# Six groups in the first set of an opening input projection: two retention jobs split 4 and 12 k tiles, one value job split 8 and 8

## What is computed

```python
mod = c @ w_ada[layer] + b_ada[layer]
sh1, sc1, gt1, sh2, sc2, gt2 = jnp.split(mod, N_MOD, axis=-1)
h = modulate(rmsnorm(x, g_mix[layer]), sh1, sc1)
proj = h @ w_in[layer]
...
qa, ka, va, qr, kr, vr, gr = jnp.split(proj, cuts, axis=-1)
ya = sliding_window_attention(qa, ka, va, sinks[layer]) * beta_attn[layer]
yr = retention(qr, kr, vr)
yr = (jax.nn.silu(gr) * head_group_norm(yr, g_ret[layer]))
y = jnp.concatenate([ya, yr], axis=-1) @ w_out[layer]
x = x + gt1[:, None, :] * y
h2 = modulate(rmsnorm(x, g_ffn[layer]), sh2, sc2)
f = jnp.square(jax.nn.relu(h2 @ w1[layer])) @ w2[layer]
x = x + gt2[:, None, :] * f
return rmsnorm(x, g_final)
```

## Time and profile before

| what | value |
|---|---|
| median of three runs | 1176.98 us |
| lowest, highest | 1175.03, 1178.56 us |
| span of the profiled execution (its time from first to last instruction) | 1176.1 us |
| TensorE busy | 1132.5 us, 96% of the span |
| VectorE busy | 795.4 us, 68% |
| ScalarE busy | 492.5 us, 42% |
| loaded from memory | 300.36 MB |

### The profile page before, as it was taken

The page is one execution under the profiler, slowest core; times in us unless marked ns, Lnnn a source line. Parts: engine busy times, 40 slices in busy tenths (PEclk is TensorE's granted clock), DMA queues, the critical chain, the costliest instruction groups (busy, mean ns, idle before and its releaser), DMA issues.

```text
span 1176.1 us, 15924 instructions
## 1 busy us (share of the span) xinstructions
PE 1132.5 (96%) x6339; PEld 957.8 (81%) x6339; DVE 795.4 (68%) x690; ACT 492.5 (42%) x517; POOL 21.1 (2%) x27
## 2 busy tenths in 40 slices
PE   3879999999999999999999999999999999999996
PEld 1769989788778878888888888888888888888885
DVE  2577889987878898866565566565566565565675
ACT  2424454555534445443333444333444333444451
POOL 2000010000000001000000000000000000000000
PEclk9999999999999998999999999999999999999999
DMA  9999989999997956766666676666676666665551
GB/s 351 368 348 397 381 319 339 338 403 390 357 404 269 322 182 223 252 222 229 235 230 185 188 222 228 235 228 186 187 220 229 238 224 187 187 196 180 180 177 72
DMA packets 156749, 303.10 MB, mean 258 GB/s; under 512 B 5425, under 2 KB 73633, under 8 KB 148129
## 3 DMA queue, kind: packets, MB, share of 16 engines
q1 hardware_dynamic: 155248, 298.08, 72.4%
q10 hardware_dynamic: 832, 2.93, 0.6%
q0 software_dynamic: 624, 1.48, 0.4%
HBM read 300.36 MB, written 2.10 MB: 257 GB/s over the span
## 4 chain that ended last, share of the span: by engine, by line
PE 91%; DVE 4%; DMA 3%; issue 1%; ACT 1%; ACTq 0%; SPq 0%; DVEq 0%
PE ps_job L924 20%; PE ps_job L963 14%; PE ps_job L964 14%; PE ps_job L965 14%; PE ps_job L927 10%; PE ps_job L939 3%; PE ps_job L940 3%; PE ps_job L941 3%; DMA stage<-in_w_ada 2%; PE ps L1030 1%; DVE acc L1247 1%; DVE w_lo L1323 1%; DMA cst<-in_consts 1%; PE ps_job L1211 1%; PE ps_job L1209 1%
## 5 line engine op out<-in xcount | busy, mean ns | idle before, releaser
L1323 DVE TENSOR_TENSOR w_lo<-stage,w_hi 128x2048 fp32r<-128x2048 f32 x164 | 375.8, 2292 | 218.5 <-ACT w_hi L518 218.3
L518 ACT ACTIVATE w_hi<-stage 128x2048 fp32r<-128x2048 f32 (+1 forms) x167 | 318.0, 1904 | 424.0 <-PE ps_job L965 231.4
L924 PE MATMUL ps_job<-act_hl,w_hi 128*128 128x512 f32 x1024 | 322.4, 396 | 1.5 <-DVE w_lo L1323 1.1
L927 PEld LDWEIGHTS ps_job<-act_hl,w_lo 128*128 128x128 f32 x1024 | 192.7, 188 | 45.0
L927 PE MATMUL ps_job<-act_hl,w_lo 128*128 128x256 f32 x1024 | 201.2, 278 | 0.0
L963 PE MATMUL ps_job<-w_hi,hid_hl 128*128 128x512 f32 x480 | 188.1, 392 | 0.0
L964 PE MATMUL ps_job<-w_lo,hid_hl 128*128 128x512 f32 x480 | 187.0, 390 | 0.0
L965 PE MATMUL ps_job<-w_hi,hid_hl 128*128 128x512 f32 x480 | 186.9, 389 | 0.0
L924 PEld LDWEIGHTS ps_job<-act_hl,w_hi 128*128 128x128 f32 x1024 | 156.1, 189 | 2.5 <-DVE w_lo L1323 1.3
L1247 DVE SCALAR_TENSOR_TENSOR acc<-stage,small,acc 128x2048 f32<-128x2048 f32 (+1 forms) x56 | 122.9, 2195 | 7.2 <-DMA stage<-in_w_ada 3.5
L963 PEld LDWEIGHTS ps_job<-w_hi,hid_hl 128*128 128x128 f32 x480 | 90.1, 188 | 19.2 <-issue 0.7
(11 more groups left out here) (223 smaller groups left out, 1127.1 us busy)
## 6 DMA issues: line engine op xcount, KB each, us to landing
stage<-in_w SPq DMA_DIRECT2D x128, 1024.0 KB, 5.3
stage<-in_w_ada SPq DMA_DIRECT2D x64, 1024.0 KB, 7.8
stage<-in_w_in SPq DMA_DIRECT2D x41, 1024.0 KB, 8.5
stage<-in_w_ada SPq DMA_DIRECT2D x32, 512.0 KB, 6.9
stage<-in_w_out SPq DMA_DIRECT2D x16, 1024.0 KB, 7.7
gate_rows<-in_w_ada SPq DMA_DIRECT2D x16, 1024.0 KB, 7.0
x_sb<-in_x ACTq DMA_DIRECT2D x1, 2048.0 KB, 13.5
out_y<-f_acc SPq DMA_DIRECT2D x3, 512.0 KB, 2.7
```

The source lines that it names most:

```text
L518: nc.scalar.activation(w_hi[:, ring, 0:width], stage[:, slot, 0:width], ACT.Copy).then_inc(hi_ready, 1)
L924: nc.tensor.matmul(ps_job[:, 2 * pair + e, :], w_hi[:, ring, ws], act_hl[:, kt, :], start=(kt == 0), stop=False)
L927: last = nc.tensor.matmul(ps_job[:, 2 * pair + e, T:2 * T], w_lo[:, ring, ws], act_hl[:, kt, 0:T], start=False, stop=(kt == KT - 1))
L1323: nc.vector.tensor_tensor(w_lo[:, ring, 0:width], stage[:, slot, 0:width], w_hi[:, ring, 0:width].bitcast(F32), ALU.subtract).then_inc(lo_ ...
```

## The change

The two wide jobs on the columns `QR0 + 512` and `QR0 + 1024` are cut at k tile 4 instead of 8: their first part is one group on k tiles 0 to 3 and moves into the first set, their second part is three groups on k tiles 4 to 15 in the second pass. The first set becomes g0 to g5: key and value, the two moved ones, then the two query jobs and `QR0`. The value job of full depth becomes two jobs of 8 k tiles, g18 and g19 of the first pass and g25 and g26 of the second; its single ACT copy becomes an ACT copy and a DVE add. Both passes keep their number of groups (20 and 23), and the number of wide and tok groups over both is unchanged (24 and 16); the first pass has two wide groups less and two tok groups more, the second pass the reverse. All tiles of the second segment now stand ahead of g5; the third segment is spread over 13 groups (g7 to g19) instead of 15. `sum_second` is called with h = g + 1 instead of g + 2, and no longer once ahead of the loop.

```diff
+SET_K = 4
+EARLY = (1, 2)
+def w_in_jobs(second):
+    k0 = HALF if second else 0
+    early = [("wide", QR0 + TOK_COLS * n, 0, SET_K) for n in EARLY]
+    jobs = [] if second else early
+    jobs += [("feat", KV0, k0, HALF)] + [("wide", Q0 + TOK_COLS * n, k0, HALF) for n in range(2)]
+    if second:
+        jobs += [("tok", VR0 + TOK_COLS, k0, HALF)]
+        jobs += [("wide", QR0 + TOK_COLS * n, SET_K, KT - SET_K) if n in EARLY else ("wide", QR0 + TOK_COLS * n, k0, HALF) for n in range(4)]
+    else:
+        jobs += [("wide", QR0 + TOK_COLS * n, k0, HALF) for n in range(4) if n not in EARLY]
     jobs += [("tok", GR0 + TOK_COLS * n, k0, HALF) for n in range(2)]
+    jobs += [("tok", VR0, k0, HALF)]
+    return jobs if second else jobs + [("tok", VR0 + TOK_COLS, k0, HALF)]
...
+FIRST_SET = [(j, 0) for j in [J_KV, *range(J_KV), *range(J_KV + 1, J_CLOSED)]]
+GROUPS = FIRST_SET + [(j, 1) for j in range(J_KV, J_CLOSED)] + [(j, q) for j in range(J_CLOSED, len(JOBS)) for q in range(N_GROUPS[j])]
+G_SET = len(FIRST_SET)
...
 def tiles_before(g):
-    second = min(KT, (0, 2, 6, 9)[g] if g < OPEN else KT)
+    second = (0, 1, 4, 7, 11, KT)[g] if g < G_SET else KT
...
-    return KT + second + min(KT, max(0, 16 * (g - OPEN) // 15)) + later
+    return KT + second + min(KT, max(0, 16 * (g - G_SET) // (G_B - 1 - G_SET))) + later
...
-            if j in (1, 2):
-                return [0, 1] if j == 1 else [4, 5]
-            if j in (0, OPEN - 1):
-                return [2] if j == 0 else [6, 7]
+            if j < J_CLOSED:
+                return [[0, 1], [4, 5], [2], [0, 1], [4, 5], [6, 7]][j]
...
-                if g - 2 == LAST_GROUP[J_V]:
-                    act.wait_ge(evacuated, J_V)
-                    act.wait_ge(group_used, LAST_GROUP[J_V] + 1)
-                    nc.scalar.activation(result_of(J_V), psum_of(J_V), ACT.Copy).then_inc(evacuated, 1)
...
             pe.wait_ge(mod_ready, 1)
-            sum_second(1)
...
-                if g + 2 <= OPEN:
-                    sum_second(g + 2)
+                if g < G_SET - 1:
+                    sum_second(g + 1)
```

More of the change, by code:

```diff
@@ L46 @@
 HALF = KT // 2
[L49 to L53, removed]
+SET_K = 4
[10 more added lines that the diff above has]
+        jobs += [("wide", QR0 + TOK_COLS * n, k0, HALF) for n in range(4) if n not in EARLY]
     jobs += [("tok", GR0 + TOK_COLS * n, k0, HALF) for n in range(2)]
-    return jobs + [("tok", VR0, k0, HALF)]
-JOBS = w_in_jobs(0, []) + w_in_jobs(HALF, [("tok", VR0 + TOK_COLS, 0, KT)])
+    jobs += [("tok", VR0, k0, HALF)]
+    return jobs if second else jobs + [("tok", VR0 + TOK_COLS, k0, HALF)]
+JOBS = w_in_jobs(False) + w_in_jobs(True)
 JOBS += [("out_attn", TOK_COLS * n, 0, HALF) for n in range(STRIPS)]
 JOBS += [("out_ret", TOK_COLS * n, HALF, HALF) for n in range(STRIPS)]
-J_B = len(w_in_jobs(0, []))
+J_B = len(w_in_jobs(False))
 J_BQ, J_BGR = J_B + 1, J_B + 8
 J_OA = J_BGR + 3
-J_V = next(j for j, job in enumerate(JOBS) if job[1:] == (VR0 + TOK_COLS, 0, KT))
 J_OR = J_OA + STRIPS
 J_MLP = J_OR + STRIPS
-OPEN = 4
-N_GROUPS = [2] + [nk // (8 if kind == "feat" else 4) for kind, _, _, nk in JOBS[1:]]
-GROUPS = [(j, q) for q in range(2) for j in range(OPEN)] + [(j, q) for j in range(OPEN, len(JOBS)) for q in range(N_GROUPS[j])]
+J_KV = len(EARLY)
+J_CLOSED = J_KV + 4
+N_GROUPS = [2 if j == J_KV else nk // (8 if kind == "feat" else 4) for j, (kind, _, _, nk) in enumerate(JOBS)]
+FIRST_SET = [(j, 0) for j in [J_KV, *range(J_KV), *range(J_KV + 1, J_CLOSED)]]
+GROUPS = FIRST_SET + [(j, 1) for j in range(J_KV, J_CLOSED)] + [(j, q) for j in range(J_CLOSED, len(JOBS)) for q in range(N_GROUPS[j])]
+G_SET = len(FIRST_SET)
 FIRST = [GROUPS.index((j, 0)) for j in range(len(JOBS))]
@@ L88 @@
 CHUNKS_BEFORE = [0, 2, 4, 8]
-OPENING = [0, OPEN, G_B]
+OPENING = [0, G_SET, G_B]
 HEAD_COLS = 2 * FEAT_COLS
@@ L665, in _ @@
                     keep_attn_part(LAST_GROUP.index(g - 2))
[L666 to L670 removed]
+                if g == G_SET:
                     modulate_segment(1)
@@ L1091, in _ @@
                     pe.wait_ge(ret_ready, 4 * q + 4)
-                if g in (2, 3):
-                    pe.wait_ge(turned_out, 2 * g + 2)
+                if g == 2:
+                    pe.wait_ge(turned_out, 6)
+                if g == G_SET - 1:
+                    pe.wait_ge(turned_out, 8)
                 if kind == "feat":
@@ L1096, in _ @@
                 elif kind == "wide":
-                    wide_group(k0 + 4 * q, (g - G_MLP) % 2, banks(j)[0], q == 0, q == N_GROUPS[j] - 1, g == OPEN - 1)
+                    wide_group(k0 + 4 * q, (g - G_MLP) % 2, banks(j)[0], q == 0, q == N_GROUPS[j] - 1, g == G_SET - 1)
                 else:
@@ L1527, in take_out @@
                 dve.wait_ge(group_used, LAST_GROUP[j] + 1)
-                if j in (J_B, J_V + 1):
+                if j == J_B:
                     dve.wait_ge(evacuated, j)
@@ L1538, in _ @@
                         add_rows(ITEMS[i][1] // 2)
-                if g == OPEN:
+                if g == G_SET:
                     copy_quarters(1, ps_job[:, 3, :], 2 * P)
@@ L1551, in _ @@
                     attention_tail(pair_at(g, 8))
-                if g - 2 in LAST_GROUP[J_B:J_OA] and g - 2 != LAST_GROUP[J_V]:
+                if g - 2 in LAST_GROUP[J_B:J_OA]:
                     take_out(LAST_GROUP.index(g - 2))
```

## The result

The changed kernel takes 1184.56 us (median of four runs, 1182.86 to 1185.26), the kernel before 1177.77 us in the same session: ratio 1.0058, interval [1.004, 1.0076]. It is slower by more than the 0.3% that can be told from no change. Its profiled span is 1182.6 us against 1176.1, so 6.5 of the some 6.8 us are to be found in the trace.

The account below looks back on a forecast made before the run. TensorE bounds the kernel (busy 1132.5 of 1176.1 us), so shifts from the opening pass through one for one. Opening 1.3, restarts 0.8, clock 1.6 and third segment 1.0 sum to 4.7 us: 1181.7 us, range 1175.5 to 1186.5.

Parts of the forecast that it names:

- main step: Opening: even tiles hold slots until the group ahead is multiplied, delaying SP's later loads; the opening costs 1.3 us.
- Its test: Opening: g3's load issued before 48 us would show the slot step wrong; the forecast had it issued at 50.15.
- Restarts: Opening: extra lag when loads restart after holes in the queue, put at 0.8 us, at most 8.
- the lag that the prediction took as its upper bound: Opening: the tile after a hole lands 4.0 us behind the first, not 1.36; three such holes, up to 8 us.
- The row of the MLP's loads: Profile row from the MLP: 1 MB loads into an empty queue land 5.3 us after issue in the median, without lag.
- Clock: Opening: half-clock fall in g4 hidden, one in g5 on the path, 1.6 us, bounds 0 and 3.2.
- The rule behind it: TensorE in the opening: waits of 2.8 and 3.0 us are long enough to cost the clock, 1.6 is not.
- Third segment: First pass, g7 to g19: paired tile sums on DVE make TensorE wait 0.8 at g15, 0.2 at g11; together 1.0 us.
- What costs nothing: Both passes: wide and tok groups changing places, ACT's two copies, DVE's add of 1.2 us; put at no cost.
- The smooth restart: Opening: restarts without lag and no clock fall in g5; 2.3 us slower, 1179.3 us, chance 0.33.
- The second rival: Opening: slots do not hold the loads, bytes alone bind; not slower, 1174.8 us, chance 0.09.
- The third: First pass becomes bound by transfers, g19's remainder 3.5 us late at 351 GB/s; 1185.2 us, chance 0.06.

Follow-up runs that it names:

- two-by-two table: Four kernels, ratios to before, sums one group ahead / right ahead of their group: four groups 1 / 1.0046, six groups 1.0021 / 1.0058.
- e1_sums_ahead: Changed kernel with TensorE's tile sums one group earlier again (sum_second(g + 2), and sum_second(1) ahead of the loop), lists unchanged: 1179.87 us, 1.0021 of before.
- e8_third_behind: e5_tiles_behind with no third-segment tile ahead of g6 or g7, two each ahead of g10, g12, g16 and g19: 1174.69 us, 0.9988 of before.
- e5_tiles_behind: e4_third with g5's load right behind g4's and the second segment's last tiles (t28 to t31) behind g5: 1173.17 us, 0.9969 of before.
- e9_before_behind: Kernel before, four groups, no third-segment tile ahead of g4 and g5, two each ahead of g8, g11 and at g19: 1175.05 us, 0.9983 of before.
- e2_dve_sums: Changed kernel with all sixteen second-segment tiles summed by DVE, none by TensorE, lists unchanged: 1179.3 us, 1.0016 of before.
- e7_before_late: Kernel before, four groups, with the second segment's even tiles between g0 and g3 summed one group later: 1182.14 us, 1.0046 of before.
- e4_third: e1_sums_ahead with third-segment tiles moved: two ahead of g6, none ahead of g7, second ones ahead of g10 and g19 only: 1175.47 us, 0.9986 of before.
- e3_clock_fill: Changed kernel with unneeded matmuls in TensorE's waits ahead of g4, g5 and g7 (24, 36, 18): 1181.44 us, 1.0038 of before.

## Why the prediction was right, and where it was not

**Direction and main step: right.** The step that carried it (an even tile holds its slot until the group ahead of it is multiplied, and every later load stands behind that slot) is what the two-by-two table isolates: 4.4 us with six groups, 5.4 with four. Its test, g3 issued before 48 us, came out at 50.13, predicted 50.15. The times it worked out hold up to g3: g1 at 43.49 (43.65), g3 at 59.54 behind a wait of 1.63 (59.7; 1.6).

**Restarts: mis-sized.** The term was 0.8 us; g5 started 3.1 late (82.63 for 79.5), and that is all of the miss in the opening. Most of it is the lag that the prediction took as its upper bound, by DVE's row at 68.38, and that came back once: t29, issued at 66.18, landed at 70.5, 0.7 later than put; t30 came 3.7 us behind it in place of 1.36. So t31 landed at 75.6 where 72.5 was put, as DVE's wait for it shows, and g5 behind it, in ACT's row:

```profile
75.63 1.28 DVE L1255 SCALAR_TENSOR_TENSOR acc<-stage,small,acc 128x1024 f32<-128x1024 f32 x1 [2.61 <-DMA stage<-in_w_ada]
...
78.34 2.86 ACT L529 ACTIVATE w_hi<-stage 128x2048 fp32r<-128x2048 f32 x2 [9.51 <-DMA stage<-in_w_in]
```

The row of the MLP's loads, for which the term was kept small, has no such lag; the row of the opening itself was the nearer one. The prediction also gave t29 the 3.6 us of a load into an empty queue, and this queue was not empty: t28, issued at 60.90, took 8.3 us to land, so it was on its way until 69.2. From there the queue ran on at half its pace. The rows that the 3.6 came from were no such case either: in before, t29 was on its way until 62.5, past t30's issue at 60.73, and t31 was issued at 62.11, not right behind t30. Section 6 for that one issue, and the window behind:

```profile
stage<-in_w_ada SPq DMA_DIRECT2D x1, 512.0 KB, 8.3
```

```profile
69.20:73.20 4.00, 2.91 (x13) 2.91 (x14) 3.61 (x3) 0.00 (x0) 0.00 (x0) 0.50 0.74 191
```

Adding to each issue its time to landing shows what the queue lost at each restart against its pace of 2.72 us for 1 MB: 2.6 us at g3, 2.7 over t25, t26 and g4, 2.3 over t29 and t30. The landings that the prediction worked out come to 2.4, 1.7 and 0.4. So a restart cost the queue much the same each time, also where a load was still on its way. The wait ahead of g4 was 3.74 for 2.8, of which the later g5 left nothing to see.

**Clock: right in size and place.** A fall in g4, hidden, and one in g5 on the path: from g5's start to g6's 9.9 us, predicted 8.4 and 1.6. The rule behind it, that the length of a wait tells whether a fall follows, is weaker than the prediction had it: the 2.72 ahead of g7 in `e1_sums_ahead` was followed by none. That each of the three long waits had its fall was in part luck.

**Opening in all:** 1.3 + 3.1 + 1.6 = 6.0, where 1.3 + 0.8 + 1.6 = 3.7 was put.

**Third segment: right, though the totals hide it.** Put at 1.0. From g6 to the second pass the shift against before grows only from 6.0 to 6.4 (175.82 against 169.37). But the first pass has two tok groups in place of two wide ones, and a tok group takes 5.44 us, a wide one 5.76: that takes off 0.6. So the doubles cost 1.1. At g15 it is 0.9 where 0.8 was put (g14 and g15 take 6.23 and 5.58 us), at g11 0.2 as put (g10 and g11 take 5.91 and 5.85). TensorE's starts of g13, g14 and g15:

```profile
134.66 0.39 PE L969 MATMUL ps_job<-w_hi,act_hl 128*128 128x512 f32 x1
...
140.10 0.39 PE L969 MATMUL ps_job<-w_hi,act_hl 128*128 128x512 f32 x1
...
146.33 0.50 PE L969 MATMUL ps_job<-w_hi,act_hl 128*128 128x512 f32 x1 [0.63 <-DVE w_lo L1331]
```

**What costs nothing:** nearly so. The prediction did not see that tok and wide groups differ; the second pass, with two wide groups more and two tok groups less, gives 0.5 of the 0.6 back (a shift of 7.0 at its end, 337.58 against 330.62). Between 420 and 480 us, behind the input projection, the changed kernel then makes up 0.4, which no run explains. So 6.0 + 1.1 - 0.1 - 0.4 = 6.6 is what the trace has (6.5 by the spans) for the sum that was put at 4.7.

**The rivals.** The smooth restart was the wrong side of the mis-sized term. The second rival (slots do not hold) named its condition, t18's sum ahead of g1's matmuls; `e1_sums_ahead` met it and got 1179.87, not the 1174.8 worked out for it, mainly because the slot of g4 holds g5 as well. The third (bound by transfers) did not come about in the changed kernel, but it is what took the gain of `e8_third_behind`. The 358 GB/s cited there as the limit of memory for one core (the Trainium skill, DMA: Bandwidth & Descriptors, Specifications) did not bind here: the queue of that kernel kept 396 GB/s for 61 us.

**What stays open.** Why a restart costs the queue 2 to 3 us even where a load is still on its way, and which load pays, no run told apart. Twice the second load paid, 3.7 to 4.0 us behind the first (t31 behind t30 in before, t30 behind t29 in the changed kernel); there the first had been issued 1.7 and 3.1 us before the last load landed. At g3 (50.13) and t25 (57.54), issued when nothing or 0.3 us of it was left, the first load paid most. But g5 in `e1_sums_ahead`, issued 3.2 us before the last load landed, paid by itself, so this is no rule. Nor was it tried whether matmuls that fill the two waits of `e5_tiles_behind` would win its clock back.

## What to carry to other kernels

In a ring of slots that is loaded in order, ask of each load which use frees its slot and where that use stands in its engine's own order: moving a sum behind a group's matmuls, or a group's load into another group's slot, delays every load behind it. Work moved into waits wins nothing if the waits are for loads that the same order holds up. Here the order of tiles, sums and loads was worth 10.5 us between kernels with the same six groups (ratios 1.0058 and 0.9969), while the best orders tried with four and with six groups (0.9983 and 0.9969) could not be told apart. Where a step is freed early, look at what the queue does meanwhile, or the gain is handed back to the transfers.

## What the runs showed of the hardware

All that follows is from 40 to 104 us, one trace of each kernel. The falls of the clock to the lower level came during or behind waits of TensorE of 1.94 us (`e9_before_behind`) to 5.59 us (`e2_dve_sums`), and lasted 3.3 to 6.8 us, or 10.3 where waits of 2.30, 1.60 and 3.12 stood in a row (`e7_before_late`). The reverse does not hold: 2.72 us ahead of g7 in `e1_sums_ahead`, and 2.18 and 2.72 in `e2_dve_sums`, were followed by none. A wait of 1.6 or 1.7 us by itself was not followed by a fall (g7 in `e4_third`, g5 in `e9_before_behind`). A stretch of 3.3 us at the lower level cost 1.5 us, and matmuls that do nothing else, put into the waits, had it back (g5 and g7 of `e3_clock_fill`).

A 1 MB load issued when the queue had run dry landed in 5.1 us (50.13 to 55.23), close to the 5.3 of the earlier trace rows. Each of three restarts in the changed kernel cost the queue 2.3 to 2.7 us against its pace, whether it had run dry or still had a load on its way.
